# Value projection in seven products, and the weight sums of the up-projection on VectorE with the first convolution tap on ScalarE

## What is computed

```python
def _project(h, w_in, a2_f, ab_f, a2_b, ab_b):
    p = jnp.einsum('bld,de->ble', h, w_in)
    u, q, k, v, g, gates, lr = jnp.split(p, IN_SPLITS, axis=-1)
...
```

```python
def conv_geglu_ffn(h, w_up, conv_w, w_down):
    up = causal_depthwise_conv(h @ w_up, conv_w)
    gate, val = jnp.split(up, 2, axis=-1)
    return (jax.nn.gelu(gate, approximate=True) * val) @ w_down
```

## Time and profile before

| what | value |
|---|---|
| median of three runs | 1770.36 us (1769.17, 1770.36, 1772.99) |
| profiled execution, its own time | 1767.6 us |
| its span in the trace | 1765.8 us |
| granted TensorE clock, mean | 0.998 |
| value projection with the modulation pieces in it | 65.65 to 133.12 us |
| up-projection in seven products, layer 0, up to the first piece of the down-projection | 1120.65 to 1227.85 us |
| the same, layer 1 | 1566.91 to 1674.11 us |

### The profile page before, as it was taken

The page is one execution under the profiler, slowest core; times in us unless marked ns, Lnnn a source line. Parts: engine busy times, 40 slices in busy tenths (PEclk is TensorE's granted clock), DMA queues, the critical chain, the costliest instruction groups (busy, mean ns, idle before and its releaser), DMA issues.

```text
span 1765.8 us, 25399 instructions
## 1 busy us (share of the span) xinstructions
PE 1714.2 (97%) x10916; PEld 1324.1 (75%) x10916; DVE 733.4 (42%) x1391; ACT 319.6 (18%) x527; POOL 181.5 (10%) x130
## 2 busy tenths in 40 slices
PE   6999999999999999999999999999999999999998
PEld 3447898974454545454698989999899898999988
DVE  3007513151111111111269544698146944469922
ACT  2004302030000000000125222111011522211101
POOL 1200000000000000000102110352000221044300
PEclk9999999999999999999999999999999999999999
DMA  9763313638999999999542123445434212335541
GB/s 381 285 247 106 134 51 140 238 147 344 428 428 428 428 428 428 428 428 428 197 144 96 49 96 96 144 157 178 167 115 143 96 49 96 96 119 168 172 162 48
DMA packets 116857, 375.79 MB, mean 213 GB/s; under 512 B 12730, under 2 KB 62242, under 8 KB 101280
## 3 DMA queue, kind: packets, MB, share of 16 engines
q1 hardware_dynamic: 115380, 373.54, 55.0%
q0 software_dynamic: 1216, 0.89, 0.2%
q10 hardware_dynamic: 172, 0.05, 0.0%
HBM read 373.41 MB, written 1.05 MB: 212 GB/s over the span
## 4 chain that ended last, share of the span: by engine, by line
PE 76%; DMA 15%; DVE 6%; ACT 1%; issue 1%; SPq 0%; DVEq 0%
PE PS L583 26%; DMA ring<-in_moe_w_dram 15%; PE PS L1362 13%; PE PS L904 8%; PE PS L1416 6%; PE PS L1326 3%; PE PS L1301 3%; PE PS L1437 2%; PE PS L935 2%; PE PS L804 2%; PE PS L1016 1%; PE PS L618 1%; DVE arena L2410 1%; PE PS L877 1%; PE PS L1025 1%
## 5 line engine op out<-in xcount | busy, mean ns | idle before, releaser
L583 PE MATMUL PS<-arena,ring 128*128 128x256 f32 (+1 forms) x1344 | 311.3, 392 | 4.4 <-DVE arena L2048 3.3
L583 PEld LDWEIGHTS PS<-arena,ring 128*128 128x128 f32 x1344 | 254.1, 190 | 56.2 <-issue 18.0
L904 PE MATMUL PS<-ring,arena 128*64 128x512 f32 x1024 | 225.1, 593 | 7.7 <-DMA ring<-in_moe_w_dram 6.6
L1362 PE MATMUL PS<-arena,ring 128*128 128x128 f32 x2016 | 226.1, 275 | 0.0
L1362 PEld LDWEIGHTS PS<-arena,ring 128*128 128x128 f32 x2016 | 225.9, 192 | 0.2
L904 PEld LDWEIGHTS PS<-ring,arena 128*64 128x64 f32 x1024 | 74.2, 137 | 155.4 <-issue 155.3
L935 PE MATMUL PS<-ring,arena 128*64 128x512 f32 x512 | 113.4, 595 | 0.5 <-ACT arena L1773 0.5
L1416 PE MATMUL PS<-arena,ring 128*128 128x256 f32 x512 | 111.5, 379 | 0.0
L1416 PEld LDWEIGHTS PS<-arena,ring 128*128 128x128 f32 x512 | 96.9, 190 | 12.9
L2328 DVE TENSOR_TENSOR arena<-arena,PS 128x512 f32<-128x512 f32 x16 | 16.8, 1052 | 214.9 <-PE PS L904 214.9
L583 PE MATMUL PS<-arena 128*128 128x128 f32 (+3 forms) x704 | 87.3, 282 | 6.8 <-DVE arena L2621 3.2
(11 more groups left out here) (408 smaller groups left out, 1980.3 us busy)
## 6 DMA issues: line engine op xcount, KB each, us to landing
ring<-in_moe_w_dram SPq DMA_DIRECT2D x96, 2048.0 KB, 16.5
ring<-in_w_in_dram SPq DMA_DIRECT2D x23, 2048.0 KB, 8.4
ring<-in_ffn_w_up_dram SPq DMA_DIRECT2D x44, 1024.0 KB, 7.5
ring<-in_w_mod_dram SPq DMA_DIRECT2D x24, 1024.0 KB, 10.0
ring<-in_ffn_w_down_dram SPq DMA_DIRECT2D x10, 2048.0 KB, 7.8
ring<-in_w_out_dram SPq DMA_DIRECT2D x4, 2048.0 KB, 7.9
ring<-in_w_gla_br_dram SPq DMA_DIRECT2D x2, 2048.0 KB, 7.8
ring<-in_w_o_dram SPq DMA_DIRECT2D x2, 2048.0 KB, 8.3
```

The lines of the kernel that those rows point to most:

```text
L583: last = mm(PS[:, b, place] if not isinstance(place, tuple) else PS[place[0], b, place[1]], lhsT(k), rhs(k), start=(k == 0), stop=(k == K ...
L904: last = mm(PS[e * SLOTS:(e + 1) * SLOTS, 4 + j, :], hg[:, k, e * SLOTS:(e + 1) * SLOTS], expert_slab(2 * j + e, KT)[:, k, :], start=(k == ...
L1362: last = mm(PS[:, b, th(i)], w4[:, k, th(i)], b4[:, k, :], start=(first and i == 0 and k == 0), stop=(end and i == 1 and k == 3), skip_gro ...
```

## The change

The value projection is put in the same seven-product form. Blocks: context tokens and x tokens by the two halves of the contraction, and the two halves of the contraction by the two value slabs. VectorE makes four weight sums of 128x2048 (after its second and third copy of k), and four token sums of 128x1024 (after the `colsL` work). TensorE runs seven `v_product`s, each over two token tiles with 4 k-tiles of 512 columns, with the modulation pieces between them as before. ScalarE saves six partial results and copies the last two, VectorE makes six additions out of PSUM.

In the up-projection VectorE makes all four weight sums; GpSimd keeps only the token sums. The first tap of each convolution becomes a ScalarE copy with a scale by column (`first_taps`), ordered by the new semaphore `tapped`; VectorE runs the two later taps (`later_taps`), the value half first. `up_products` and `weights_summed_late` go; `sum_products` and `weights_summed` count both stages.

```diff
+            def v_product(bank, tokens, weights, first=False, end=False, waits=lambda t: None):
+                for t in range(TT):
+                    waits(t)
+                    b = ph1.hold(pe, (bank, t)) if first else ph1.place((bank, t))
+                    for k in range(4):
+                        last = mm(PS[:, b, :], tokens[:, k, th(t)], weights[:, k, :], start=(first and k == 0),
+                                  stop=(end and k == 3), skip_group_check=True)
+                    last.then_inc(S("sum_products"), 1)
...
             for j in range(2):
-                w = slab("v", j)
-                for t in range(4):
-                    tiles(ph1, ("v", j, t), [(slice(0, 512), lambda k: hboth[:, k, t * P:(t + 1) * P],
-                                              lambda k: w[:, k, :])], KT)
-                    if j == 0:
-                        modulation(1, range(2 * t, 2 * t + 2))
-                    elif t == 0:
-                        modulation_turned(1)
-                    elif t == 1:
-                        modulation(2, range(4))
-                last_unit1[where1[("v", j)]] = ("v", j, 3)
+                slab("v", j)
+            v_product("vA", h_quarter(0, 0), v_quarter(0, 0), first=True)
+            modulation(1, range(2))
+            v_product("vB", h_quarter(0, 1), v_quarter(1, 0), first=True, end=True)
+            modulation(1, range(2, 4))
+            sums_made(1)
+            v_product("vD", v_tokens[0], v_weights[0], first=True)
+            modulation(1, range(4, 6))
+            sums_made(2)
+            v_product("vA", v_tokens[1], v_weights[1], waits=lambda t: pe.wait_ge(S("held_copied"), 1 + t))
+            modulation(1, range(6, 8))
+            sums_made(3)
+            v_product("vA", v_tokens[2], v_weights[2], waits=lambda t: pe.wait_ge(S("held_copied"), 5 + t))
+            modulation_turned(1)
+            pe.wait_ge(S("weights_summed"), 4)
+            v_product("vA", h_quarter(1, 1), v_weights[3], end=True, waits=lambda t: pe.wait_ge(S("fourth_read"), 1 + t))
+            modulation(2, range(4))
+            pe.wait_ge(S("tokens_summed"), 4)
+            v_product("vD", v_tokens[3], v_quarter(1, 1), end=True, waits=lambda t: pe.wait_ge(S("held_copied"), 3 + t))
...
+                    if SL1[i - 3][0] == "v":
+                        sp.wait_ge(S("sum_products"), 14 if SL1[i - 3][1] else 4)
+                        sp.wait_ge(S("weights_summed"), 4)
...
+                def first_taps(m, v):
+                    for i in range(2):
+                        ins = A(gcv[:, m % 2, 2 * v + i, :], upc[:, m % 2, 2 * v + i, :], ACT.Copy,
+                                scale=ffn_tap(FFN_CONV - 1, FFT * v + 2 * m + i))
+                    ins.then_inc(S("tapped"), 1)
...
             for h in range(GH):
                 b = ph1.read(dve, ("k", 0, h))
                 V.tensor_copy(kT[:, h, :], PS[:, b, :]).then_inc(psum_free[b], 1)
+                if h == 1:
+                    for j in range(2):
+                        dve.wait_ge(wl[1 + j], 32 + 16)
+                    v_weight_sum(0, v_quarter(0, 1), v_quarter(0, 0), ALU.subtract)
+                    v_weight_sum(1, v_quarter(1, 1), v_weights[0], ALU.subtract)
+                elif h == 2:
+                    v_weight_sum(2, v_quarter(1, 1), v_quarter(0, 1), ALU.subtract)
+                    dve.wait_ge(S("weights_summed"), 2)
+                    v_weight_sum(3, v_quarter(1, 0), v_weights[1], ALU.subtract)
...
+            v_token_sum(0, h_quarter(1, 0), h_quarter(1, 1), ALU.add)
+            dve.wait_ge(S("tokens_summed"), 1)
+            v_token_sum(1, v_tokens[0], h_quarter(0, 0), ALU.subtract)
+            v_token_sum(2, h_quarter(0, 0), h_quarter(1, 0), ALU.subtract)
+            v_added("vB", 3, 1, 0, 0, True)
+            dve.wait_ge(S("sum_products"), 6)
+            dve.wait_ge(S("tokens_summed"), 2)
+            v_token_sum(3, h_quarter(0, 1), v_tokens[1], ALU.subtract)
+            v_added("vA", 9, 3, 2, 1, False)
             modulate(1)
+            v_added("vD", 13, 5, 0, 1, True)
...
                 for j in range(FIRST_SUMMED):
+                    if j:
+                        weight_sum(FIRST_SUMMED, 1)
+                        weight_sum(FIRST_SUMMED, 2)
...
                 for j in range(FIRST_SUMMED, FFT // 2 + 2):
                     m = j - 2
                     if m >= FIRST_SUMMED:
                         dve.wait_ge(S("held_copied"), held_due(m, 3))
-                        dve.wait_ge(S("up_products"), products_due("three", m))
+                        dve.wait_ge(S("sum_products"), products_due("three", m))
                         b = ph3.place(("D", m))
                         V.tensor_tensor(upc[:, m % 2, 0:2, th(1)], held[:, 2, m % 2], two(b), ALU.add).then_inc(psum_free[b], 1)
...
+                        dve.wait_ge(S("tapped"), due("tapped", 2 * (m - FIRST_SUMMED) + 1))
+                        link(later_taps(m, 1))
+                        dve.wait_ge(S("tapped"), due("tapped", 2 * (m - FIRST_SUMMED) + 2))
+                        later_taps(m, 0).then_inc(S("value_conv"), 1)
...
                     if j < FFT // 2:
+                        weight_sum(j, 3)
...
                     if m >= FIRST_SUMMED:
                         gate(m)
+                    if j < FFT // 2:
+                        weight_sum(j, 4)
+                    if j < LAST_UP:
+                        weight_sum(j + 1, 1)
+                        weight_sum(j + 1, 2)
```

More of the change, by code:

```diff
@@ L717, in _ @@
                     ph1.freed(pe, ("krc", d, t))
+            for t in range(TT):
+                ph1.freed(pe, ("vB", t))
+                ph1.freed(pe, ("vD", t))
             for d in range(2):
@@ L738, in _ @@
                     ph1.freed(pe, ("krx", d, t))
+            for t in range(TT):
+                ph1.freed(pe, ("vA", t))
+            pe.wait_ge(S("fourth_read"), 2)
             for h in range(GH):
@@ L1565, in _ @@
                             n = SL3[before][1] - FIRST_SUMMED + 1
[L1566 to L1568 removed]
+                            sp.wait_ge(S("sum_products"), products_due("four", SL3[before][1]))
+                            sp.wait_ge(S("weights_summed"), due("weights_summed", 4 * n))
                         else:
@@ new lines, in _, with hold @@
+                for j in range(FIRST_SUMMED, FFT // 2 + 2):
+                    m = j - 2
+                    if m >= FIRST_SUMMED:
+                        ph3.freed(act, ("D", m))
+                        first_taps(m, 0)
+                    def hold(n, step, at):
+                        act.wait_ge(S("sum_products"), products_due(step, j))
+                        A(held[:, n, j % 2], two(ph3.place((at, j))), ACT.Copy).then_inc(S("held_copied"), 1)
+                    if j < FFT // 2:
+                        hold(0, "one", "A")
+                    if m >= FIRST_SUMMED:
+                        act.wait_ge(S("value_conv"), due("value_conv", m - FIRST_SUMMED + 1))
+                        gelu(m)
+                    if j < FFT // 2:
+                        hold(1, "five", "D")
+                        hold(2, "six", "A")
@@ L2049, in _, with v_weight_sum @@
                     .then_inc(S("h1_tokens"), 1)
+            def v_weight_sum(n, a, b, op):
+                if n % 2:
+                    dve.wait_ge(S("weights_summed"), n)
+                V.tensor_tensor(v_weights[n], a, b, op).then_inc(S("weights_summed"), 1)
             for h in range(GH):
@@ L2061, in _, with v_token_sum, v_added @@
                 .then_inc(S("cols_ready"), 1)
+            def v_token_sum(n, a, b, op):
+                V.tensor_tensor(v_tokens[n], a, b, op).then_inc(S("tokens_summed"), 1)
+            def v_added(bank, at, held, tile, j, frees):
+                for t in range(TT):
+                    dve.wait_ge(S("held_copied"), held + t)
+                    dve.wait_ge(S("sum_products"), at + t)
+                    b = ph1.place((bank, t))
+                    place = vtok[:, tile + t, j * 512:(j + 1) * 512]
+                    ins = V.tensor_tensor(place, PS[:, b, :], place, ALU.add)
+                    ins.then_inc(psum_free[b] if frees else S("fourth_read"), 1)
+            v_token_sum(0, h_quarter(1, 0), h_quarter(1, 1), ALU.add)
[7 more added lines that the diff above has]
+            v_added("vA", 9, 3, 2, 1, False)
             modulate(1)
+            v_added("vD", 13, 5, 0, 1, True)
             dve.wait_ge(S("lb_ready"), 1)
```

132 lines of the change are left out of this document (68 added, 64 removed).

## The result

| | before | after |
|---|---|---|
| median of seven runs each | 1772.97 us (1767.92 to 1775.58) | 1761.3 us (1759.73 to 1764.38) |
| profiled execution, own time | 1767.6 us | 1759.73 us |
| its span, mean granted clock | 1765.8 us, 0.998 | 1757.9 us, 0.999 |

The ratio after to before is 0.9942 [0.9929, 0.9955], a gain of 0.58%, which is 10.3 us (8.0 to 12.6) of 1772.97; the two medians lie 11.7 us apart. The forecast was 7.0 us of gain and 1763.4 us; the time lies in the range and 2.1 us under the forecast. The sign and the main term held; 3 to 5 us of the gain were not in the sum. The two profiled executions differ by only 7.9 us, so the missing part is not between these two traces, and that is the question which most of the experiments are about.

The account below looks back on a forecast made before the run. TensorE, busy 1714.2 of 1765.8 us, was taken as the bound. The value projection gives -6.97 us, the up-projection 0, so the median goes from 1770.36 to 1763.4 us; range 1760.0 to 1768.2.

Parts of the forecast that it names:

- the main term: Value projection: TensorE runs seven products instead of eight, saving 6.97 us on the path.
- Value projection: TensorE's value stage loses one of eight products, 6.97 us; the added VectorE work costs nothing on the path.
- lr: TensorE's next stage after the value products, forecast to start at 126.2 us instead of 133.12, without idle in front.
- The covers: Value stage: VectorE's sums finish before TensorE needs them, by 20 us for weight sums and 12 us for token sums.
- The additions out of PSUM: Value stage: VectorE's additions of partial products, at most 1.05 us each, nothing on the path.
- The tightest: VectorE's addition before product six adds into bank vA: done at 109.4 us, needed at 112.4, slack 3.0 us.
- Up-projection: VectorE's period becomes 10.44 of 12.51 us; path price 0 and no gain, since TensorE never waited.
- The base: Starting time of the forecast: 1770.36 us, the median of three runs, from which 7.0 us was taken.
- Rival (a): VectorE's first value weight sums hold GpSimd's parameter issues, delaying TensorE's transposes: 0 to 6.6 us lost; chance 0.10.
- Rival (b): Up-projection: over 2.1 us added to VectorE's period makes it the bound; 1 us over gives 1777 us; chance 0.06.
- Rival (c): Last modulation slab lands late, beyond 1.2 us slack; 2 us more landing time costs 0.8 us, 1764.2; chance 0.05.
- Rival (d): Value products: split accumulation costs TensorE 0.3 us at each of 14 groups, eating 4 us: 1767.6; chance 0.04.

Follow-up runs that it names:

- the kernel with the first half alone: Only the value projection changed, the up-projection left as in the kernel before: 1763.48 us, ratio 0.9957 to the kernel before.
- the kernel with one sum more: Kernel before, with VectorE making the fourth weight sum twice in each of the nine summed up-projection pairs: 1790.37 us, ratio 1.0102.
- all three kernels with room: Kernel before with the up-projection's edit whole (ratio 0.9975), only its sums moved to VectorE (0.9976), or only its first taps moved to ScalarE (0.9979).
- the sharper form with two more sums: Kernel after, with two extra 128x2048 VectorE sums behind the first copy of k, beside GpSimd's transfer issues: 1759.86 us, ratio 0.9941 to the kernel before.
- the kernel with the second half alone: Only the up-projection changed, the value projection left as in the kernel before: 1767.93 us, ratio 0.9975 to the kernel before.

## Why the prediction was right, and where it was not

**Value projection: right.** Forecast 6.97 us; the stage shortened by 6.86, and the doubled product costs 6.97 in the trace. "lr" was to start at 126.2 us and starts at 126.36. The covers held: the weight sums run at 52.08 and 54.40 (2.28 and 2.29 us, 2.29 forecast), the second pair ends at 63.6 (63.8 forecast), the token sums at 70.5 (70.8). The additions out of PSUM were priced at most 1.05 us, by a row of the same shape with both kinds of reading; they take 0.69. The tightest ends at 109.3, and product six's second half begins at 108.76 + 3.5 = 112.3, so the slack is the 3.0 us of the forecast.

**Up-projection: the prices right, the term wrong.** VectorE's new period was put at 10.44 us and is 9.77 busy; ScalarE's at 4.05 and is 3.98. L1362 (now L1398) stayed at 0.0 idle, as forecast. The step that failed is "VectorE ... is 12.35 of 12.60 us busy ... though nobody waits for it there" and, out of it, "Price on the path: 0, and no gain either, since TensorE never waited". That was true of the one execution that had been profiled. Over the runs the term is -4.4 us (-2.5 to -6.2) instead of 0. It comes from executions of the kernel before in which GpSimd's sums fall on VectorE's taps. One such execution stands in a trace, with 5.2 us lost, and the kernel with the first half alone has a milder one, with 1.0 us lost (a stage of 108.2 us instead of 107.2). In these and in the kernel with one sum more every wait of the products for that addition stands behind four stretched taps (3.9 to 5.95 us). That the other long executions lose in the same way is inferred from the two groups of times at one clock, the upper of which is missing in all three kernels with room.

**The base.** The forecast was made on 1770.36 us, a median of three runs; seven gave 1772.97. The gain was taken too small, by 4.7 us of the medians, and the base too low, by 2.6 us, and the two misses partly cancelled: 1763.4 against 1761.3. That the time came out as near as 2.1 us is in part luck.

**Rival (a), parameters late: did not occur.** GpSimd's issues beside the weight sums keep 0.48 to 0.53 us, the last at 55.07 (55.19 before); in the sharper form with two more sums they kept their length too. TensorE idled 0.35 us in front of the transposes there, but 0.2 us also in the kernel with the up-projection's half alone, which has no sums beside the issues. The rival's price failed as well: it carried a delay of the issue into the landing one to one, and where an issue did come 3.9 us later the landing did not move. The reason that the prediction gave for taking 0 was poor, though: it leaned on one-input copies that "ran beside the issues with no visible trace". Those were copies out of PSUM of 0.69 us. Here it was the copy inside SBUF that held the issues, and the two-input sum that didn't.

**Rival (b), VectorE over the period: not with this kernel.** The point from which it decides was put at 2.1 us; two extra sums (2.45 us) cost nothing and four (4.9 us) make VectorE the bound, so the point lies between, as the idle 12.51 - 9.77 = 2.74 us say. The mechanism, VectorE late for TensorE, was right and stood on the wrong side: it was the kernel *before* in which it came from time to time.

**Rival (c), modulation slab late: did not occur.** SP issues the last four from 116.85 us over 2.90 us, and modulation(2) starts at 128.10 without idle time. **Rival (d), split accumulation: did not occur.** From its start to the next piece's, each product takes 6.96 to 7.07 us, as the tiles did before, and the up-projection 107.36.

**Open.** All kernels, the one after too, scatter by 4 to 5 us from run to run (1759.7 to 1764.4) with the mean clock between 0.999 and 0.995. The traces show what this part is made of. In the kernel with the second half alone (span 1763.8 us, clock 0.999) and in the one with the sums alone moved (1767.9 us, 0.995), the k projection took 29.23 and 30.32 us, the eight 128x512 products before the expert stage 3.60 and 5.27, and a piece in layer 1 behind a wait of 2.43 us:

```profile
1381.75 3.72 PE L583 MATMUL PS<-arena,cst 128*128 128x256 f32 x16 [2.43 <-ACT arena L1851]
```
```profile
1384.25 5.41 PE L583 MATMUL PS<-arena,cst 128*128 128x256 f32 x16 [2.43 <-ACT arena L1851]
```

These three pieces, each behind a wait of TensorE and the slower ones at a granted clock of 0.50 to 0.68, differ by 4.5 us together; the spans differ by 4.1. Why the clock falls there in one execution and not in another stays open. So does whether the change has a part in it: the eight products were slow in 5 of the 7 traces whose value stage is 67.5 us long and in none of the 7 in which it is 60.6.

## What to carry to other kernels

An engine that is nearly full in a period although nobody waits for it, and whose work contends with another's, is not priced by one trace: look at how its idle time changes from period to period, ask what happens if its contended work slides in front of the instruction that the bound engine wants, and look at the spread of the runs, which here was twice as wide as that of a kernel with room. Moving two contending streams onto one engine can make the period shorter, and steadier, than dividing them between two: with all the sums and taps on VectorE it was idle 1.3 us a period, with two sums on GpSimd 0 to 1.2. When one block product is taken out of a stage whose bound is TensorE, the gain is that product's time and no more.

## What the runs showed of the hardware that was not expected

- Two-input float32 work of VectorE and GpSimd on SBUF was nearly serialised: four taps went from 1.79 to 5.85 us beside 4.9 us of GpSimd's sums, a 128x512 gate from 0.68 to 2.84, a 128x1024 sum from 1.23 to 3.37, and GpSimd's own sum from 2.35 to 3.2 and 3.4.
- A wait of 3.3 us on TensorE was followed by 5.7 us at a granted clock of 0.70, which added half of the wait again.
- Copies inside SBUF on VectorE stretched GpSimd's transfer issues from 0.5 to 1.3 us; sums of the same size left them alone. The last transfer, issued 3.9 us later, landed at the same 65.3 us.
